# Both ends of a loop of block products: low parts moved from GpSimd to VectorE, and the order of the conversions around the loop

## The reference

```python
h = modulate(rms_norm(x, g_pre_ffn), sh2, sc2)
f = (jax.nn.silu(h @ w_gate) * (h @ w_up)) @ w_down     # inner width 2816
x = x + gt2[:, None] * rms_norm(f, g_post_ffn)
```

## Time and profile before

| what | value |
|---|---|
| device time, three runs | 993.98 us (992.97 to 995.07) |
| the profiled execution: device time, span | 994.06 us, 992.2 us |
| PE busy | 927.7 us, 93% of the span |
| DVE, ACT, POOL busy | 592.1, 463.5, 352.2 us |
| mean granted TensorE clock | 0.982 |

### The profile page before, as it was taken

One profiled execution on the slowest core, in us unless ns is written; L12 is line 12 of the kernel. 1 busy time (PEld: TensorE's weight loads), 2 busy tenths in 40 slices (PEclk: granted clock), 3 DMA queues, 4 the chain that ended last, 5 costly groups with the idle time before them and its releaser, 6 DMA issues. The chain is left out here.

```text
span 992.2 us, 17662 instructions
## 1 busy us (share of the span) xinstructions
PE 927.7 (93%) x6864; PEld 879.1 (89%) x6864; DVE 592.1 (60%) x1095; ACT 463.5 (47%) x895; POOL 352.2 (35%) x199
## 2 busy tenths in 40 slices
PE   3899999899999999999999898999999994999995
PEld 1698898899998999988888797999999994999995
DVE  5767558988884333333100799999999988100005
ACT  4755326465557555443433764445444446222121
POOL 2031016456363231244445073433333332434450
PEclk9999999999999999999999999999999997999998
DMA  9831022232231113357865202223222222122202
GB/s 362 321 108 48 8 94 84 104 108 74 87 105 51 43 47 140 116 226 266 302 205 186 86 1 85 87 85 108 107 87 86 87 71 89 59 89 88 88 30 96
DMA packets 35619, 111.84 MB, mean 113 GB/s; under 512 B 4240, under 2 KB 9360, under 8 KB 35280
## 3 DMA queue, kind: packets, MB, share of 16 engines
q1 hardware_dynamic: 31152, 102.48, 29.6%
q10 hardware_dynamic: 4112, 6.93, 1.9%
q0 software_dynamic: 272, 1.31, 0.3%
HBM read 100.38 MB, written 10.32 MB: 112 GB/s over the span
## 5 line engine op out<-in xcount | busy, mean ns | idle before, releaser
L1296 POOL TENSOR_TENSOR wlo<-raw,whi 128x1024 fp32r<-128x1024 f32 x53 | 132.4, 2498 | 233.2 <-ACT whi L868 223.8
L1930 PE MATMUL pj<-hh,whi 128*128 128x288 f32 x544 | 124.3, 310 | 5.1 <-ACT zs L949 2.4
L1930 PE MATMUL pj<-hh,wlo 128*128 128x288 f32 x544 | 117.0, 297 | 0.0
L1930 PE MATMUL pj<-hl,whi 128*128 128x288 f32 x544 | 116.6, 296 | 0.0
L1353 POOL TENSOR_TENSOR op_lo<-ssum,op_hi 128x512 fp32r<-128x512 f32 x42 | 57.4, 1387 | 142.0 <-PE pj L2184 142.0
L1930 PEld LDWEIGHTS pj<-hh,whi 128*128 128x128 f32 x544 | 86.6, 191 | 7.9 <-issue 3.8
L1930 PEld LDWEIGHTS pj<-hl,whi 128*128 128x128 f32 x544 | 87.8, 189 | 0.0
L1930 PEld LDWEIGHTS pj<-hh,wlo 128*128 128x128 f32 x544 | 87.8, 189 | 0.0
L1365 POOL TENSOR_TENSOR dlo<-rawd,dhi 128x1408 fp32r<-128x1408 f32 x16 | 51.5, 3220 | 92.3 <-ACT dhi L1245 91.9
L1185 ACT ACTIVATE op_hi<-ssum 128x512 fp32r<-128x512 f32 x80 | 50.2, 628 | 71.4 <-DVE ssum L1692 54.2
L1868 DVE RECIPROCAL rstd<-rms 128x288 f32<-128x288 f32 x2 | 3.9, 1952 | 127.2 <-ACT rms L1123 127.2
(11 more groups left out here) (289 smaller groups left out, 2763.3 us busy)
## 6 DMA issues: line engine op xcount, KB each, us to landing
raw<-in_w_s SPq DMA_DIRECT2D x54, 512.0 KB, 4.1
sraw<-in_w_s SPq DMA_DIRECT2D x40, 512.0 KB, 4.2
rawa<-in_w_ada SPq DMA_DIRECT2D x32, 512.0 KB, 6.0
rawd<-in_w_d SPq DMA_DIRECT2D x16, 704.0 KB, 4.0
raw<-in_w_ada SPq DMA_DIRECT2D x16, 512.0 KB, 10.3
g_raw<-gz ACTq DMA_DIRECT2D x16, 288.0 KB, 2.1
gate<-g_raw SPq DMA_DIRECT2D x8, 576.0 KB, 3.7
rawv<-in_w_v SPq DMA_DIRECT2D x8, 324.0 KB, 5.3
```

What stands on the lines that cost most here:

```text
L1296: pool.tensor_tensor(rest, raw_of(c), whole.bitcast(F32), ALU.subtract).then_inc(w_lo, 1)
L1930: ins = mm(pj[tile % 2][:, h, 0:HALF], w[:, slot(c), b:b + P], x[:, kc, h * HALF:(h + 1) * HALF], start=(kc == first and w is whi and x is ...
```

## The change

1. **Low parts of pair 0.** POOL makes three of them (3, 4, 5), as in the other pairs. DVE makes the four others, between the steps of `t_rest` and the standard chunks.
2. **ACT's order ahead of the loop.** The high parts 3, 4, 5 of pair 0 now come ahead of 1, 2, 6 (`HI_FIRST`).
3. **DVE's order ahead of the loop.** T3 (`t_make(1)`) goes behind `first_half(1)`; T4 (`t_make(3)`) and the low part of T1 go behind the instructions that free the `pj` banks of the third chunk, T4 and T3's low part behind those of the fourth. S1 and S2 of pair 1 go behind the last standard chunk's `f_made`.
4. **The seam.** The first `rawd` half is loaded once pair 18 has its low parts (before: pair 19), the second as before. `dlo` of d = 0 is made on DVE (`down_rest`, semaphore `d_lo_vec`). DVE's order becomes: 1 `fl`, `dlo` half 0, 5 `fl`, the last `combine`, 2 `fl`, `dlo` half 1, 6 `fl`, the last `f_made`, 8 `fl`. ACT's order: 1 `fh`, `dhi` half 0, 5 `fh`, `dhi` half 1, 4 `fh`, the last silu, 12 `fh`. SP waits on `d_lo_vec` for the loads of d = 1.

```diff
 def wait_operand_lo(eng, i, k):
-    by_pool = i == 0 or k in POOL_LO
+    by_pool = k in POOL_LO
...
+def wait_down_lo(eng, d, k):
+    if d:
+        eng.wait_ge(d_lo, 2 * (d - 1) + k + 1)
+    else:
+        eng.wait_ge(d_lo_vec, k + 1)
...
 for d in range(KC):                      # SP
     for k in range(2):
-        if d:
-            sp.wait_ge(d_lo, 2 * (d - 1) + k + 1)
+        if d == 0:
+            wait_pair_lo(sp, N_PAIR - 2 + k)
+        elif d == 1:
+            sp.wait_ge(d_lo_vec, k + 1)
         else:
-            wait_pair_lo(sp, N_PAIR - 1)
+            sp.wait_ge(d_lo, 2 * (d - 2) + k + 1)
...
 inverse(rstd2, 1, 0)                     # DVE
 first_half(0)
 t_make(0)
-t_make(1)
 inverse(rstd2, 1, 1)
 first_half(1)
+t_make(1)
 t_make(2)
...
-rest_of_f(0, 8)                          # DVE, seam
+rest_of_f(0, 1)
+down_rest(0)
+rest_of_f(1, 6)
 combine(N_PAIR - 1)
-rest_of_f(8, 12)
+rest_of_f(6, 8)
+down_rest(1)
+rest_of_f(8, 14)
 v.wait_ge(up_ready, N_PAIR)
 f_made(FC - 1, gt, up)
-rest_of_f(12, FC)
+rest_of_f(14, FC)
```

## The result

| | kernel before | changed kernel |
|---|---|---|
| median of 5 runs each, side by side, us | 993.62 (992.97 to 995.07) | 978.20 (977.59 to 979.71) |
| ratio, 95% interval | | 0.9845 (0.9831 to 0.9860) |
| profiled execution, us | 994.06 | 977.59 |
| its span, us | 992.2 | 975.8 |
| its mean granted clock | 0.982 | 0.988 |

The forecast was 979.6 us, from 976.8 to 983.4. To see where the 16.4 us of span went, I cut both traces at four rows: ACT's `rms` ahead of the front, `gbuf` of pair 0 on DVE, PE's first matmul of the down projection, PE's first matmul of its last tile.

The account below looks back on a forecast made before the run. PE leads the chain of waits; its waits at the loop's two ends, 17.2 us, are all ended by DVE, which takes turns with POOL. 994.06 - 2.4 (front) - 10.6 (seam) - 2.7 (clock) + 1.2 (collision) = 979.6 us, range 976.8 to 983.4.

Parts of the forecast that it names:

- front: Ahead of the loop: 5.8 us fewer turns, less 2.4 added low parts and 1.1 idle; `gbuf` starts 2.4 us earlier.
- seam, PE's start earlier: At the seam: PE starts at 824.4 instead of 835.0, 10.6 us earlier; its wait shrinks from 12.6 to 2.0 us.
- clock: Behind the seam wait: granted clock stays 1.00 instead of falling to 0.50, gaining 2.7 us.
- collision at tile 0's end: End of tile 0: POOL's first `dlo` holds up DVE's `fl` 21, so PE loses 1.2 us at block 21.
- the two turns in pair 1 stay: Front, pair 1: DVE still waits for POOL twice, at S4 and the low part behind it, 2.2 us.
- rival 2: Turns fall DVE's way: front gives 3.5 (978.5), or POOL's `dlo` misses the last two `fl` (978.4), both 977.3; chance 0.14.
- behind 3.1 us it stayed 1.00, so behind 2.0 us I expect it to stay: Seam: granted clock expected to stay 1.00, as behind the wait ahead of product (0, 3); worth 2.7 us.
- 0.50 behind either wait: Sign of being wrong: granted clock 0.50 behind PE's remaining wait at (1, 1), 2.4 us, or at the seam, 2.0 us.
- rival 1: Clock falls after all: at the front 982.3, at the seam 981.1, at both 983.8 us; chance 0.22.
- it takes its turn: End of tile 0: POOL's `dlo` gets its turn for about 3.05 us from 838.0, while DVE has `fl` left.
- should DVE get `fl` 20 through first, 21 still waits: End of tile 0: even then 1.2 us is lost; 0 only if POOL came 1 us later.
- Rivals 3 to 5: Seam pulled forward less, 981.2 or 983.6 (0.06); front gives nothing, 982.0 (0.04); more turns in steady pairs, 1001 (0.02).

## Why the prediction was right, and where its terms were off

| step | predicted | measured | |
|---|---|---|---|
| ahead of the front | 0 | 0.36 | scatter of the start |
| front | 2.4 | 3.3 | one turn fell DVE's way |
| seam, PE's start earlier | 10.6 | 10.7 | right |
| clock | 2.7 | 2.7 in the profile, 1.2 usually | the fall was the rule |
| collision at tile 0's end | 1.2 lost | 0.6 lost, or 0 | another engine waited |
| time, us | 979.6 | 977.59 in the profile, 978.2 median | |

The 2.7 us are the 2.07 us from the seam to the last tile, with the 0.6 of the new wait added back. Where the clock falls, that stretch takes 124.3 us instead of 125.56, a gain of 1.2, and nothing is lost at tile 1. The working then gives 994.06 less 0.36, 3.3, 10.7 and 1.2, or 978.5, near the median of 978.2. **The time was close because errors of opposite sign met**: the clock's gain was put 1.5 us too high, the front's 0.9 too low, and the collision's 1.2 us are not there. That the sum fell so near the median is in part luck.

- *Front.* The mechanism held step by step: 1.03 us idle for the root (1.1 predicted), T3 2.08 and T2 2.46 (2.0 and 2.4), T2's and T1's low parts 1.36 (1.35), PE's wait gone at (0, 3). Wrong was the step "the two turns in pair 1 stay". POOL and DVE's S4 came at 603.10 together; S4 kept its 0.69 us, POOL's two took 3.51 instead of 2.55, and only the next DVE instruction waited 1.1. This is the first half of rival 2 (978.5), which I had given 0.14 with its second half. As DVE was that much earlier, the wait ahead of (1, 1) stayed 1.5 instead of growing to 2.4. The Trainium skill (SBUF — State Buffer, SBUF: two separate sides) lets whoever starts first hold the port pair. The experiment with tile 0's `dlo` on POOL agrees, where DVE comes to a running POOL instruction (two `fl` held, 5.6 us); in pair 1 both came at 603.10, and the row, not the rule, tells who was first.
- *Seam.* Every term came out: `dlo` on DVE 1.63 us (1.6), the five `fl` 3.43 us (5 x 0.67), the wait 1.94 (2.0). The load of half 0 was no longer waited for.
- *Clock.* The step "behind 3.1 us it stayed 1.00, so behind 2.0 us I expect it to stay" failed as a rule. It took one profile's row as the behaviour of the kernel. The same 3.1 us wait in the same code showed 1.00 in one profile and 0.63 over 4 us in another. The sign that I had named, 0.50 behind either wait, is absent from the first profile of the changed kernel and present in its second (0.50 from 822 to 824). My 0.22 for rival 1 was too small, and its price was wrong too: it put 2.7 us on a fall, taken from the stretch behind the 12.6 us, and gave 981.1 for the seam, where a fall behind 1.9 us cost 1.5 us and the median was 978.2. Nor is the 2.7 fixed: behind the same 12.6 us, with the front alone changed, the clock cost 2.0. The range, said to take in rival 1, ended at 983.4, below the 983.8 of its case with both falls.
- *Collision.* The step "it takes its turn" failed: POOL waited for DVE through to the end of the `fl`. The case that I had dismissed ("should DVE get `fl` 20 through first, 21 still waits") assumed that POOL gets in between two of DVE's instructions. It did not in any profile with a POOL `dlo` at this place.
- *Rivals 3 to 5* are excluded by the rows: `dlo` 1.63, `dhi` not waiting for its load, the front worth 3.0 us alone, and 215.27 us from `gbuf` to the seam, which leaves no room for turns added in the pairs.

What stays open is what decides a turn. POOL, out of a long idle time, lost to the whole row of `fl` at the end of tile 0 in every profile with a `dlo` there, but got in after one DVE instruction in pair 1, and at 818.41, 0.9 us after its last instruction, after a part of one `fl`. Whether it is the length of DVE's unbroken stream, what its instructions read, or POOL's own start, these runs do not tell. Nor do they tell why the clock was kept once in eight.

## What to carry to other kernels

Work that two engines do by turns is best counted as the waiting it puts on the engine that PE waits for: here 1.63 us of DVE's own work ahead of `up`, and as much behind it, replaced 5.6 us of stalls ahead of `up`, and four low parts more on DVE made it earlier. A wait that is taken away pays only up to the next one, so list for each place what is late next: 2.0 us at the seam came back in full as waits when the `combine` alone was moved. With every `dlo` on DVE and the later table load beside it, the same move was worth 2.1 us from `rms` to the last tile (362.77 against 364.85), the clock included. A granted clock read in one profile behind a short gap is one draw; cost it both ways, and prefer the edit that leaves no gap.

## What the runs showed that I had not expected

- The granted clock can fall behind a gap of 1.9 us of PE, and did in seven of eight profiles at the seam; it cost 1.5 us over the next 80 matmuls, as much as behind 6.57 us. Behind 12.6 us it cost 2.0 and 2.7. Two profiles of one kernel, in which the front and the seam stood 0.01 us apart, differed in it, and at another place 1.92 us cost nothing.
- A POOL instruction can wait through several DVE instructions in a row: 1.2, 1.7 and 2.8 us, each time to the end of the unbroken row of `fl`, though a POOL instruction that runs holds DVE for its whole length.
- A slower PE can make DVE faster: with the clock down in pair 0, POOL woke 1.3 us later behind `rms`, and DVE met two turns less, 2.2 us.
